# First mixer's attention in a three-block layer: values held still in the array, results by channel instead of by token

## The reference, cut to what matters

```python
def forgetting_attention(q, k, v, logf, valid):
    c = jnp.cumsum(logf, axis=-1)
    def block(i):                       # 128 queries at a time
        logits = jnp.einsum('bhqd,bhkd->bhqk', qb, k) * scale + cb[..., None] - c[:, :, None, :]
        allowed = (kpos[None, :] <= qpos[:, None]) & (valid[None, :] | (kpos[None, :] == qpos[:, None]))
        p = jax.nn.softmax(jnp.where(allowed[None, None], logits, NEG), axis=-1)
        return jnp.einsum('bhqk,bhkd->bhqd', p, v)
...
y_a = y_a.transpose(0, 2, 1, 3).reshape(B, P, FOX_W)
mixed = g_a * (y_a @ w_o_fox) + g_b * (y_b @ w_o_ret)
```

## Time and profile before

| | us |
|---|---|
| median of 3 runs (lowest, highest) | 3765.16 (3762.26, 3765.64) |
| profiled execution: time, span | 3762.98, 3761.1 |
| PE busy | 3699.8 (98% of the span) |
| DVE, ACT, POOL busy | 1379.1, 747.7, 1045.5 |
| granted TensorE clock, mean | 0.993 |

### The profile page before, as it was taken

The page is one execution under the profiler, slowest core; times in us unless marked ns, Lnnn a source line. Parts: engine busy times, 40 slices in busy tenths (PEclk is TensorE's granted clock), DMA queues, the critical chain, the costliest instruction groups (busy, mean ns, idle before and its releaser), DMA issues.

```text
span 3761.1 us, 42034 instructions
## 1 busy us (share of the span) xinstructions
PE 3699.8 (98%) x17561; PEld 2623.7 (70%) x17561; DVE 1379.1 (37%) x2219; ACT 747.7 (20%) x1327; POOL 1045.5 (28%) x919
## 2 busy tenths in 40 slices
PE   8999999999999999999999999999999999999999
PEld 7888667775554788864575444478887557858888
DVE  3221210422111322135635200178822274248851
ACT  2000251223110100012332300010012354230000
POOL 4544100000000355423441000146640020016653
PEclk9999999999999999999999999999999999999999
DMA  4322444333232232232232222233223310023322
GB/s 130 90 79 83 84 66 69 57 62 62 57 67 78 79 90 87 84 96 73 84 100 86 70 75 78 78 84 85 87 91 110 72 42 4 6 59 87 90 84 73
DMA packets 370368, 286.07 MB, mean 76 GB/s; under 512 B 11283, under 2 KB 360083, under 8 KB 370180
## 3 DMA queue, kind: packets, MB, share of 16 engines
q1 hardware_dynamic: 369892, 283.11, 28.6%
q10 hardware_dynamic: 288, 0.27, 0.0%
HBM read 280.64 MB, written 2.72 MB: 75 GB/s over the span
## 4 chain that ended last, share of the span: by engine, by line
PE 96%; DVE 1%; ACT 1%; DMA 1%; issue 1%; POOL 0%; SPq 0%; DVEq 0%; ACTq 0%
PE psum L604 42%; PE psum L1999 14%; PE psum L1319 6%; PE psum L2192 3%; PE psum L1440 3%; PE psum L2890 3%; PE psum L1354 2%; PE psum L1146 2%; PE psum L1116 2%; PE psum L3730 1%; PE psum L1986 1%; PE psum L1112 1%; PE psum L3465 1%; PE psum L573 1%; PE psum L2976 1%; PE psum L2996 1%
## 5 line engine op out<-in xcount | busy, mean ns | idle before, releaser
L604 PE MATMUL psum<-work 128*128 128x256 f32 (+1 forms) x2400 | 551.4, 381 | 0.0
L523 POOL TENSOR_TENSOR work<-weight_ring 128x512 f32<-128x512 f32 x132 | 163.1, 1236 | 1378.5 <-PE psum L604 735.7
L604 PEld LDWEIGHTS psum<-work 128*128 128x128 f32 x2400 | 456.0, 190 | 66.0
L604 PE MATMUL psum<-work,weight_ring 128*128 128x256 f32 (+1 forms) x2080 | 481.8, 381 | 0.0
L604 PE MATMUL psum<-normalized,weight_ring 128*128 128x256 f32 (+1 forms) x2016 | 469.5, 383 | 2.7 <-DVE normalized L724 2.7
L1999 PE MATMUL psum<-normalized,weight_ring 128*128 128x512 f32 x1024 | 450.5, 596 | 0.0
L604 PEld LDWEIGHTS psum<-work,weight_ring 128*128 128x128 f32 x2080 | 395.2, 190 | 57.2
L604 PEld LDWEIGHTS psum<-normalized,weight_ring 128*128 128x128 f32 x2016 | 384.4, 191 | 61.3 <-DVE normalized L724 4.2
L1999 PEld LDWEIGHTS psum<-normalized,weight_ring 128*128 128x128 f32 x1024 | 192.0, 191 | 228.4 <-issue 227.3
L748 DVE TENSOR_TENSOR work<-work,psum 128x512 f32<-128x512 f32 (+1 forms) x100 | 68.6, 686 | 643.3 <-PE psum L604 643.3
L682 ACT ACTIVATE work<-psum 128x256 f32<-128x256 f32 (+1 forms) x100 | 38.5, 385 | 1095.9 <-PE psum L604 1095.9
(11 more groups left out here) (514 smaller groups left out, 4757.1 us busy)
## 6 DMA issues: line engine op xcount, KB each, us to landing
weight_ring<-in_w_in SPq DMA_DIRECT2D x73, 1024.0 KB, 7.9
weight_ring<-in_w_ffn_in SPq DMA_DIRECT2D x88, 512.0 KB, 5.1
weight_ring<-in_ffn_w_up SPq DMA_DIRECT2D x44, 512.0 KB, 4.8
weight_ring<-in_ffn_up SPq DMA_DIRECT2D x44, 512.0 KB, 5.1
weight_ring<-in_w_ffn_out SPq DMA_DIRECT2D x16, 1024.0 KB, 5.2
weight_ring<-in_w_out SPq DMA_DIRECT2D x12, 1024.0 KB, 5.2
work<-decay_sums SPq DMA_DIRECT2D x16, 512.0 KB, 4.1
weight_ring<-in_w_proj_b SPq DMA_DIRECT2D x8, 1024.0 KB, 5.1
```

What stands on the lines that cost most here:

```text
L523: own(pool.tensor_tensor(s1, a21, a22, ALU.add))
L604: last = pe.matmul(K.ps[:, self.BANK[m] * T:self.BANK[m] * T + self.H], left(m, p), right(pe, m, p), start=first and p == 0, stop=last_par ...
```

## The change

The product with the values is turned round: 64 columns of a head's values are stationary and the 128x128 transposed weights move, so the result comes with channels on the partitions, head 0 of the pair on 0 to 63 and head 1 on 64 to 127, and no transpose of it is needed. The units of both heads are multiplied together on even steps (`weigh_pe`), the two heads on column halves of the array. The meta weights are transposed as four tiles of 128x32 onto 32 partitions (L1245), the meta values are a 32x128 stationary tile (L1253), and POOL's tile becomes 128x128. The divisors now belong to columns: eight matmuls per pair multiply a divisor column, repeated 64 times as stationary operand, by the identity (`spread_factors_pe`, L1264, rel 3), ACT copies them from bank 5 (rel 3), and DVE multiplies at rel 4 as before, now by a full 128x512 tile. `turn_y_pe` and its copy at rel 5 are gone.

```diff
@@ attention_pe
             self.side_until(side, (s + 4) * SIDE)
             if more and rel == 6:
                 self.meta_scores_pe(pe, p + 1)
+            if s % 2 == 0 and 4 <= s < n + 4:
+                self.weigh_pe(pe, s - 4)
             if 2 <= s < n + 2:
...
-            if 3 <= s < n + 3:
-                u = s - 3
-                pair, h, i = units[u]
-                pe.wait_ge(*S["copied"](u + 1))
...
-                for t in range(i + 1):
-                    last = pe.matmul(self.pair_bank(pair)[:, at:at + 64], A(self.pt + (u % 2) * T + t * P, P),
-                                     A(self.v + t * D + (2 * pair + h) * 64, 64), start=u % PAIR_UNITS == 0 and t == 0, stop=False,
...
                 if rel == 3:
                     self.meta_values_pe(pe, p - 1)
-                if rel == 5:
-                    self.turn_y_pe(pe, p - 1)
+                    self.spread_factors_pe(pe, p - 1)
+
+    def weigh_pe(self, pe, first):
+        pair, _, i = self.units()[first]
+        pe.wait_ge(*S["copied"](first + 2))
+        if first % PAIR_UNITS == 0 and pair > 1:
+            pe.wait_ge(*S["tails"](pair - 1))
+        for t in range(i + 1):
+            for h in range(2):
+                last = pe.matmul(self.pair_bank(pair)[half(h), i * P:(i + 1) * P], A(self.v + t * D + (2 * pair + h) * 64, 64),
+                                 A(self.pt + h * T + t * P, P), start=first % PAIR_UNITS == 0 and t == 0, stop=False, skip_group_check=True)
+        last.then_inc(S["weighed"].h, 1)
@@ meta_turn_pe
-        pe.transpose(K.bank(5, P), A(self.mm + (p % 2) * P, P), K.ident[:, :]).then_inc(S["meta_turned"].h, 1)
+        for i in range(NT):
+            last = pe.transpose(K.bank(5, P, 2 * META, i * P), A(self.mm + (p % 2) * P + i * 2 * META, 2 * META), K.ident[:, :])
@@ meta_values_pe
-        pe.matmul(self.pair_bank(p), A(self.mt + (p % 2) * P, P), A(self.vbd, T), start=False, stop=True, skip_group_check=True)\
+        rows = slice(0, 2 * META)
+        pe.matmul(self.pair_bank(p), A(self.vbd, P, rows), A(self.mt, T, rows), start=False, stop=True, skip_group_check=True)\
@@ spread_factors_pe, in place of turn_y_pe
+        pe.wait_ge(*S["inverted"](p + 1))
+        pe.wait_ge(*S["meta_copied"](p + 1))
+        for i in range(NT):
+            for h in range(2):
+                column = A(self.total + (p % 2) * PAIR_UNITS + 2 * i + h, 1).to_broadcast([P, 64])
+                last = pe.matmul(K.bank(5, P, P, i * P)[half(h)], column, K.ident[:, :], start=True, stop=True)
@@ attention_act
-                    act.activation(A(self.mt + ((p - 1) % 2) * P, P), K.bank(5, P), ACT.Copy).then_inc(S["meta_copied"].h, 1)
-                if rel == 5:
-                    act.wait_ge(*S["y_turned"](p))
-                    act.activation(A(self.q + (p - 1) * T, T), K.bank(5), ACT.Copy).then_inc(S["y_ready"].h, 1)
+                    act.activation(A(self.mt, T, slice(0, 2 * META)), K.bank(5, rows=2 * META), ACT.Copy).then_inc(S["meta_copied"].h, 1)
+                if rel == 3:
+                    act.wait_ge(*S["factors_spread"](p))
...
+                    act.activation(A(self.factors, T), K.bank(5), ACT.Copy).then_inc(S["factors_copied"].h, 1)
@@ tail_dve
-        dve.tensor_tensor(by(A(self.q + p * T, T), 64), by(self.pair_bank(p), 64),
-                          spread(A(self.total + (p % 2) * PAIR_UNITS, PAIR_UNITS), 64), ALU.mult).then_inc(S["tails"].h, 1)
+        dve.wait_ge(*S["factors_copied"](p + 1))
+        dve.tensor_tensor(A(self.q + p * T, T), self.pair_bank(p), A(self.factors, T), ALU.mult).then_inc(S["tails"].h, 1)
```

More of the change, by code:

```diff
@@ L904, in places @@
         self.L, self.pt, self.ncb = A.put(3 * T), A.put(2 * T), A.put(2 * T)
-        self.vbd, self.own_block = A.put(T), A.put(T)
+        self.vbd, self.own_head, self.factors = A.put(P), A.put(P), A.put(T)
         self.km, self.sums, self.cm = A.put(FOX_PAIRS * 2 * META), A.put(TM), A.put(FOX_HEADS * META)
-        self.mm, self.mt = A.put(2 * P), A.put(2 * P)
+        self.mm, self.mt = A.put(2 * P), A.put(T)
         self.stat_min, self.stat_sum = A.put(PAIR_UNITS * FOX_PAIRS), A.put(PAIR_UNITS * FOX_PAIRS)
@@ L929, in take_signals @@
             qk_done=8, squared=16, summed=16, rooted=16, tile_read=16, km_ready=16, v_read=4,
-            scored=64, scaled=64, probs=64, turned=64, copied=64, weighed=64,
+            scored=64, scaled=64, probs=64, turned=64, copied=64, weighed=32,
             meta_scored=8, meta_biased=8, meta_least=8, meta_less=8, meta_probs=8, meta_turned=8, meta_copied=8, vbd_ready=8, weighed_all=8,
-            sums_stored=16, row_even=16 * FOX_PAIRS, row_odd=16 * FOX_PAIRS, tails=8, y_turned=8, y_ready=8,
+            sums_stored=16, row_even=16 * FOX_PAIRS, row_odd=16 * FOX_PAIRS, tails=8, inverted=8, factors_spread=8, factors_copied=8,
             side=28, side_read_a=28, side_read_b=28, roped=8, ga_open=8,
@@ L1192, in attention_pe @@
                 last.then_inc(S["turned"].h, 1)
-            if 3 <= s < n + 3:
-                u = s - 3
-                pair, h, i = units[u]
-                pe.wait_ge(*S["copied"](u + 1))
-                if u % PAIR_UNITS == 0 and pair > 1:
-                    pe.wait_ge(*S["tails"](pair - 1))
-                at = (2 * i + h) * 64
-                for t in range(i + 1):
-                    last = pe.matmul(self.pair_bank(pair)[:, at:at + 64], A(self.pt + (u % 2) * T + t * P, P),
-                                     A(self.v + t * D + (2 * pair + h) * 64, 64), start=u % PAIR_UNITS == 0 and t == 0, stop=False,
-                                     skip_group_check=True)
-                last.then_inc(S["weighed"].h, 1)
             if s >= PAIR_UNITS:
@@ L1248, in meta_values_pe, with spread_factors_pe @@
         pe.wait_ge(*S["vbd_ready"](p + 1))
-        pe.matmul(self.pair_bank(p), A(self.mt + (p % 2) * P, P), A(self.vbd, T), start=False, stop=True, skip_group_check=True)\
+        rows = slice(0, 2 * META)
+        pe.matmul(self.pair_bank(p), A(self.vbd, P, rows), A(self.mt, T, rows), start=False, stop=True, skip_group_check=True)\
             .then_inc(S["weighed_all"].h, 1)
-    def turn_y_pe(self, pe, p):
+    def spread_factors_pe(self, pe, p):
         K, A, S = self.K, self.A, self.s
-        pe.wait_ge(*S["tails"](p + 1))
+        pe.wait_ge(*S["inverted"](p + 1))
         pe.wait_ge(*S["meta_copied"](p + 1))
-        for t in range(NT):
-            last = pe.transpose(K.bank(5, P, P, t * P), A(self.q + p * T + t * P, P), K.ident[:, :])
-        last.then_inc(S["y_turned"].h, 1)
+        for i in range(NT):
+            for h in range(2):
+                column = A(self.total + (p % 2) * PAIR_UNITS + 2 * i + h, 1).to_broadcast([P, 64])
+                last = pe.matmul(K.bank(5, P, P, i * P)[half(h)], column, K.ident[:, :], start=True, stop=True)
+        last.then_inc(S["factors_spread"].h, 1)
     def early_tiles(self):
@@ L1366, in late_side_pe @@
             yield from self.channel_tile_pe(pe, "ret_g", c, U, TM)
-        pe.wait_ge(*S["y_ready"](8))
+        pe.wait_ge(*S["tails"](8))
         for c in range(KD):
@@ L1723, in total_dve @@
         own.wait()
-        own(dve.reciprocal(total, total))
-        own.wait()
+        dve.reciprocal(total, total).then_inc(S["inverted"].h, 1)
     def tail_dve(self, dve, p):
```

19 lines of the change are left out of this document (12 added, 7 removed).

## The result

The changed kernel ("after" from here on) takes 3773.98 us (median of 9 runs, 3769.94 to 3778.57), the kernel before 3764.16 beside it (9 runs, 3761.03 to 3767.96): a ratio of 1.0024, 95% interval 1.0016 to 1.0032. It is slower by 9.8 us, or 0.26%, inside the range of 3759 to 3775, near its upper end, and just outside of what was called no change (0.2%); 3767 had been predicted.

The account below looks back on a forecast made before the run. PE's time was taken to bound the kernel, with the engine chain setting the attention's end. - 0.5 + 1.0 + 1.7 = + 2.2 us on the profiled 3762.98 gave 3765.2, about 3767 as median; range 3759 to 3775.

Parts of the forecast that it names:

- The regime and the prices: Attention until 918 us: PE's passes set the time, priced by starts in other stages' rows, 0.055 us per half-array pass.
- costed at nothing: Pairs with side tiles: longer ACT copy of meta weights and new waits on PE, ACT and DVE hidden by side tiles.
- the copy of one side tile: Pairs with side tiles: a late copy makes PE wait at most about a microsecond, in two or three of seven pairs.
- the second rival: Meta transposes in a mode of their own, two passes each plus mode changes: + 5.0 us, 3772; chance 6%.
- the third: Rival: ACT's or DVE's hold at rel 3 and 4 reaches PE, 1 us in each pair: 3775; chance 6%.
- The end chain: Last pair, last transpose to retention, without side-tile cover: 5.14 us instead of 3.43, 1.7 more.
- The last transposes come 1.0 us later: Steps 58 to 65: less even order and uncovered spreading delay the last transposes 1.0 us past 931.13.
- the - 0.5 of the pairs: Seven pairs with side tiles: PE gains 0.07 us each, - 0.5 us in all.
- My bound of 2 ("they take up nothing"): Steps 58 to 65: upper limit of 2 us on the last transposes' delay, if waits for copies take up nothing.
- The clock: Sign of being wrong: a granted clock below 1.00 in the last pair; no size given.
- The Trainium skill, TensorE: Matmul & The Clock Gate, Part 3: Rule weighed for column halves: loads overlap only across different row groups; by it the sum would be 22 us higher.

Follow-up runs that it names:

- single: Changed kernel with value products one unit at a time, in every step behind the transposes, so no two column halves run side by side: 3789.69 us, ratio 1.0064.
- all2: Changed kernel with products beside scores, late ones behind transposes, three transposed-weight buffers, stretched side tiles, divisors repeated by copy and transposed ahead of meta values: 3759.57 us.
- behind3: Changed kernel with value products behind the even step's transposes and three buffers of transposed weights instead of two: 3769.20 us, ratio 1.0011 to the kernel before.
- behind: Changed kernel with value products behind the even step's transposes instead of ahead, still two buffers of transposed weights: 3777.23 us, ratio 1.0035 to the kernel before.
- ring: Changed kernel with a fourth buffer for DVE's scaled scores where there were three: 3773.18 us, ratio 1.0024 to the kernel before.
- ahead: Changed kernel with the eight spread products moved ahead of the meta values at rel 3: 3770.26 us, ratio 1.0015 to the kernel before.
- warm: Changed kernel with twelve unread identity transposes in PE's gap ahead of the retention: 3769.11 us, ratio 1.0011 to the kernel before.
- cover_before: Kernel before with side tiles stretched to last until step 62 instead of 56, forget-sum rows fetched earlier: 3761.44 us, ratio 0.9996 to the kernel before.
- cover_after: Changed kernel with side tiles stretched to last until step 62 instead of 56, forget-sum rows fetched earlier: 3767.45 us, ratio 1.0012 to the kernel before.
- near: Changed kernel with value products directly behind the scores and side tiles behind both, one mode change less per even step: 3770.06 us, ratio 1.0017.

## Why the prediction was right and wrong

**The regime and the prices: right.** While there are side tiles the change is neutral: predicted -0.4 us up to pair 5, measured +0.46. The prices read in other stages held to 0.05 us each; what was missed is waits. Up to 918 us PE waits 2.3 us for the meta exponentials (L1245) where it waited 1.7 (L1243), which I had costed at nothing, and 1.2 us for the copy of one side tile where it waited 0.6, which I had named but not added. Single shows what a pair costs without the overlap, 3.0 us more. The meta transposes are one pass each, so the second rival is out as well; so is the third, since PE waits neither for reciprocals nor for the factor copy in pairs with side tiles.

**The end chain: right.** 5.10 for 5.14. all2 shows that its length was a matter of the form: with one-pass transposes ahead of the meta values it is about 4.

**"The last transposes come 1.0 us later": the step that failed.** Against the start of the attention they come 3.84 later (281.54 for 277.70), where + 1.0 and the - 0.5 of the pairs made + 0.5. 0.9 of the miss is from the pairs with side tiles, 2.5 from the last steps. The term of the sum that failed is this + 1.0, which should have been about + 3.4. The prediction named the place, and said that products of two units stand ahead of the transposes, but followed it with prices of passes and took the waits for copies at about their old size. In the kernel before each unit's transposes are followed by some unit's products, which lie beside ACT's copy: bank 2 is read out while PE multiplies. In the changed kernel products come on even steps only, ahead, so that the odd unit's transposes follow the even unit's with only the copy between them. Waits for copies: 0.8 before, 3.5 after, 1.1 in behind3, where products stand between again and a buffer lets the copy start. The order alone isn't what helps there: behind, with the same order and no third buffer, has 4.1. ring excludes DVE's buffers. My bound of 2 ("they take up nothing") was not a bound at all: it counted the products once, but not the copy that their absence lays open.

**The clock: listed as a thing that would prove me wrong, with no price.** I had named the last pair; in after it fell right behind, at 941.4, during PE's last wait. It costs 1.6 us: the way from the retention to its outputs, the same work in all kernels, takes 196.35 to 196.38 in the six where the half clock doesn't reach into it (before, single, ahead, behind3, all2, and warm from its own first transposes), and 197.7 to 198.7 where it does; cover_before, with 198.21, has no fall there but a wait of PE of 1.6 us for ACT.

All eleven kernels whose value products stand on two halves side by side have a stretch at half clock somewhere in the attention or right behind it; before, single and cover_before have none, though single's spreading alternates halves too. That looks like the value products' doing, but a rival fits as well: PE's own waits. Of the 16 falls between 640 and 960 us in these kernels twelve begin in a wait of PE of 1.4 to 2.9 us or within 2 us behind one, and the other four at the end of the attention in ahead, warm, behind and cover_after, behind a row of waits of about half a microsecond each. Here the wait that comes ahead of the fall at 739 in ahead, on PE's timeline, and the windows on both sides of the fall:

```profile
737.92 0.61 PE L1245 MATMUL psum<-identity,work 128*32 128x128 f32 x4 [2.44 <-ACT work L1520]
738.47 1.19 PE L1224 MATMUL psum<-work 64*128 64x256 f32 x8
739.59 4.66 PE L1361 MATMUL psum<-weight_ring,normalized 128*128 128x256 f32 x14
```

```profile
735.00:739.00 4.00, 1.56 (x11) 0.94 (x11) 2.40 (x7) 2.12 (x7) 0.00 (x0) 1.00 0.05 18
739.00:742.50 3.50, 3.50 (x13) 2.72 (x10) 1.35 (x6) 0.82 (x2) 0.00 (x0) 0.52 0.00 0
```

In the kernel before, PE's waits in the attention are at most 1.4 us long, and outside it the clock falls there too, at 591 us, behind this, where no product stands on halves:

```profile
590.43 5.81 PE L1146 MATMUL psum<-weight_ring,normalized 128*128 128x256 f32 x18 [3.64 <-DVE work L1608]
```

Neither cause is shown. The halves aren't needed for a fall, and a wait doesn't bring one each time (1.8 us at 890 in after without a fall, 1.5 in single ahead of the retention). No kernel here has the value products side by side without waits of over 1.4 us, so the two can't be told apart.

**The time in the range.** That the time still lies in the range is luck. The range reached up to 3775 for the second and third rival, and neither came true; what filled it was the waits for copies and the clock, for which the range had no room of its own beyond 2 us for the last pair.

**What stays open.** Attention and clock are 7.1 us of the 9.8 in the medians. The other 2.7 can't be placed: the stages behind show +2.5 in the one pair of profiles and differ as much between other kernels. ahead, warm and near are 4 to 5 us below after in the median (the intervals overlap), but to the outputs near has 1.5 us less than after in its profile, warm 0.9 more and ahead 2.5 more; one profile of each doesn't resolve what the medians do.

The Trainium skill, TensorE: Matmul & The Clock Gate, Part 3, would have weight loads overlap only across different row groups. The trace disagrees for column halves, now in the changed kernel itself (16 passes of 128x64 against 128x128 in 1.03 us), and single shows that what ends when the halves aren't alternated is just this overlap (8 passes in 1.02).

## What to carry to other kernels

Where stages run without cover, count for each consumer what stood beside the copy it waits for: work that moves from between two waits to ahead of both costs nothing while other work covers it, and its whole copy when none does. The number of buffers decides whether a reordering helps at all: PE's waits for copies went from 3.5 to 4.1 us with two (behind) and to 1.1 with three (behind3). Price a form from other stages' rows by starts, which held here to 0.05 us, count the way in ahead of the first start, and then repair the chain end first: the gain of the repaired form, 0.75 us a pair, reached the retention's start only when the last pair no longer gave it back.

## What the hardware showed that I had not expected

- A DVE reciprocal took 3.35 us for 128x512 and 0.20 for 128x8, while a copy that repeats 8 columns 64 times over took 0.43. Repeat after the reciprocal, not before.
- Alternated column halves run two passes in the time of one: 0.064 us a pass with the way out (1.03 for 16), 0.128 when one half is used alone (1.02 for 8).
- A load of 32 rows ahead of the meta values costs no more than 0.05 us over the plain form (1.05 from L1253 to the next start, 1.01 before), and four 128x32 transposes take 0.53 to 0.54 with the change to the next matmul's part of the array, as four of 128x128 do (757.11 to 757.64 before).
- The granted clock fell to 0.50 (1.2 GHz) for 3.4 or 6.8 us, and once for 13.7, at changing places in and right behind the attention, most often in or right behind a wait of PE of only 1.4 to 2.9 us; a stretch of 3.4 us cost about 1.6.
